# Column sums of squares on TensorE: one result column instead of 128, in a three-layer fp32 transformer kernel

## The reference

```python
def rms_norm(x, g):
    xf = x.astype(jnp.float32)
    y = xf * lax.rsqrt(jnp.mean(xf * xf, axis=-1, keepdims=True) + EPS)
    return (y * g.astype(jnp.float32)).astype(x.dtype)

# second model, each of its six sub-layers:
        h = rms_norm_2(x, g[0])
        ...
        x = x + rms_norm_2(y, g[1])
```

## Time and profile before

| | before |
|---|---|
| median of 3 runs | 2448.61 us (2446.7 to 2450.1) |
| profiled execution, its own time | 2450.1 us |
| profiled execution, span of the trace | 2448.3 us |
| mean granted TensorE clock | 0.957 |
| PE busy | 2257.6 us, 92% |
| weight loads (PEld) busy | 1836.5 us, 75% |
| DVE, ACT, POOL busy | 51%, 46%, 28% |
| mean DMA rate | 106 GB/s |

### The profile page before, as it was taken

One profiled execution on the slowest core, in us unless ns is written; L12 is line 12 of the kernel. 1 busy time (PEld: TensorE's weight loads), 2 busy tenths in 40 slices (PEclk: granted clock), 3 DMA queues, 4 the chain that ended last, 5 costly groups with the idle time before them and its releaser, 6 DMA issues.

```text
span 2448.3 us, 30850 instructions
## 1 busy us (share of the span) xinstructions
PE 2257.6 (92%) x11314; PEld 1836.5 (75%) x11314; DVE 1240.1 (51%) x2222; ACT 1118.1 (46%) x1958; POOL 680.1 (28%) x434
## 2 busy tenths in 40 slices
PE   7988899989999999988979999999987888999997
PEld 5755688867888887766867888887875777788886
DVE  6767544537999834455454322224538445323233
ACT  5445633446888725555343322223737334332221
POOL 4150033311000121401233332233922323332232
PEclk9888999989999999998989999999999889999999
DMA  4300022215999720220211322221310221223221
GB/s 159 112 18 35 10 99 97 101 47 190 391 391 384 290 86 19 75 88 1 86 61 52 104 96 95 102 95 61 104 69 1 69 70 35 95 95 104 95 95 52
DMA packets 71653, 258.92 MB, mean 106 GB/s; under 512 B 7952, under 2 KB 8080, under 8 KB 71120
## 3 DMA queue, kind: packets, MB, share of 16 engines
q1 hardware_dynamic: 66816, 238.76, 27.4%
q0 software_dynamic: 2816, 11.82, 1.3%
q10 hardware_dynamic: 1872, 6.37, 0.7%
HBM read 245.36 MB, written 11.56 MB: 105 GB/s over the span
## 4 chain that ended last, share of the span: by engine, by line
PE 78%; DVE 8%; ACT 6%; issue 4%; POOL 2%; DMA 1%; POOLq 0%; DVEq 0%; SPq 0%; ACTq 0%
PE ps L506 16%; PE ps L508 16%; PE ps L507 16%; PE ps L1108 3%; PE ps L566 3%; PE ps L1123 2%; PE ps L2669 2%; PE ps L2671 2%; PE ps L2670 2%; PE ps L542 2%; PE ps L548 2%; PE ps L543 2%; PE ps L1142 2%; PE ps L2696 1%; PE ps L2697 1%
## 5 line engine op out<-in xcount | busy, mean ns | idle before, releaser
L448 ACT ACTIVATE wh<-raw 128x1024 fp32r<-128x1024 f32 x308 | 322.4, 1055 | 484.8 <-PE ps L508 458.4
L453 DVE TENSOR_TENSOR wl<-raw,wh 128x1024 fp32r<-128x1024 f32 x180 | 242.5, 1354 | 539.8 <-ACT wh L448 533.8
L506 PE MATMUL ps<-hh,wh 128*128 128x512 f32 (+1 forms) x1192 | 469.4, 394 | 8.2 <-POOL wl L453 7.9
L508 PE MATMUL ps<-hh,wl 128*128 128x512 f32 (+1 forms) x1192 | 466.2, 391 | 0.0
L507 PE MATMUL ps<-hl,wh 128*128 128x512 f32 (+1 forms) x1192 | 466.2, 391 | 0.0
L453 POOL TENSOR_TENSOR wl<-raw,wh 128x1024 fp32r<-128x1024 f32 x128 | 309.2, 2416 | 553.0 <-ACT wh L448 543.7
L506 PE MATMUL ps<-act,wh 128*128 128x512 f32 (+1 forms) x688 | 269.5, 392 | 11.5 <-ACT act L1368 9.9
L506 PEld LDWEIGHTS ps<-hh,wh 128*128 128x128 f32 (+1 forms) x1192 | 225.0, 189 | 57.8 <-issue 10.5
L507 PE MATMUL ps<-act,wh 128*128 128x512 f32 (+1 forms) x688 | 267.4, 389 | 0.0
L508 PE MATMUL ps<-act,wl 128*128 128x512 f32 (+1 forms) x688 | 267.2, 388 | 0.0
L508 PEld LDWEIGHTS ps<-hh,wl 128*128 128x128 f32 (+1 forms) x1192 | 224.7, 189 | 47.9
(11 more groups left out here) (463 smaller groups left out, 3908.4 us busy)
## 6 DMA issues: line engine op xcount, KB each, us to landing
raw<-d_w SPq DMA_DIRECT2D x277, 512.0 KB
raw_x<-d_moe SPq DMA_DIRECT2D x84, 512.0 KB, 6.8
raw<-d_moe SPq DMA_DIRECT2D x84, 512.0 KB
d_xs<-Sb POOLq DMA_DIRECT2D x7, 514.0 KB, 7.6
Xb<-d_xs ACTq DMA_DIRECT2D x6, 514.0 KB, 6.4
area<-d_mem POOLq DMA_DIRECT2D x3, 1024.0 KB, 5.2
d_ys<-rows ACTq DMA_DIRECT2D x6, 512.0 KB, 6.2
xT<-d_x SPq DMA_DIRECT2D x8, 256.0 KB, 7.0
```

What stands on the lines that cost most here:

```text
L448: me.e.activation(hi, raw, ACT.Copy).then_inc(*me.done("wh", m))
L453: me.e.tensor_tensor(lo, raw, hi.bitcast(F32), ALU.subtract).then_inc(*me.done("wl", m))
L506: me.e.matmul(bank[0:m, 0:n], wh[:, c], hi, start=k == 0, stop=False)
L508: mm = me.e.matmul(bank[0:m, 0:n], wl[:, c], hi, start=False, stop=last)
```

## The change

`column_sums` multiplies by one column of ones (or, for two heads, by columns 0 and 64 of the block matrix) instead of 128 columns, and writes its sums side by side at the start of the PSUM bank, one column for each tile of 128 tokens (or two). `summed_columns`, which picked every 128th or 64th column, is gone; its three readers read the first columns of the bank. The number of matmuls, their stationary operands, their waits and the semaphores they raise are the same, and so is the order of instructions on every engine.

```diff
 def column_sums(K, me, acc, sq, key, first, last, rows=128, ncol=T, nh=1):
     nt = ncol // 128
-    rhs = K.ones[0:rows, :] if nh == 1 else K.blk
+    rhs = K.ones[0:rows, 0:1] if nh == 1 else K.blk[:, 0:128:64]
     for i in range(nt):
-        q = slice(128 * i, 128 * i + 128)
-        mm = me.e.matmul(acc[:, q], sq[0:rows, q], rhs, start=first and i == 0, stop=last and i == nt - 1)
+        mm = me.e.matmul(acc[:, nh * i:nh * i + nh], sq[0:rows, 128 * i:128 * i + 128], rhs, start=first and i == 0,
+                         stop=last and i == nt - 1)
     mm.then_inc(*me.done(*key))
-
-
-def summed_columns(acc, ncol=T, nh=1):
-
-    return acc[:, 0:ncol:128 // nh]
...
-    me.e.activation(s, summed_columns(acc, ncol, nh), ACT.Sqrt, bias=K.eps, scale=1.0 / width).then_inc(*me.done("root", st))
+    me.e.activation(s, acc[:, 0:ncol // 128 * nh], ACT.Sqrt, bias=K.eps, scale=1.0 / width).then_inc(*me.done("root", st))
...
-    me.e.activation(K.stat[:, i, 0:NQ], summed_columns(K.ACC), ACT.Sqrt, bias=K.eps, scale=1.0 / D).then_inc(*me.done("root", st))
+    me.e.activation(K.stat[:, i, 0:NQ], K.ACC[:, 0:NQ], ACT.Sqrt, bias=K.eps, scale=1.0 / D).then_inc(*me.done("root", st))
...
-    me.e.scalar_tensor_tensor(v.rearrange("p (i h) -> p i h", h=nh), summed_columns(acc, T, nh).rearrange("p (i h) -> p i h", h=nh),
+    me.e.scalar_tensor_tensor(v.rearrange("p (i h) -> p i h", h=nh), acc[:, 0:NQ * nh].rearrange("p (i h) -> p i h", h=nh),
                               1.0 / width, bc(K.et[:, :], nh), ALU.mult, ALU.add).then_inc(*me.done("var", st))
```

## The result

The changed kernel took 2468.69 us (median of 4 runs, 2460.8 to 2470.8), the kernel before beside it 2447.65 us (2440.45 to 2450.1). The ratio is 1.0070, 95% interval 1.0043 to 1.0098. So one result column instead of 128 costs 17 to 20 us by the two ratios. The forecast was 2485 us, 36 us slower, with a range of 2455 to 2503: the direction and the mechanism came as forecast, the size at about half.

What follows compares the result with a forecast made beforehand. The prediction took PE to bound the kernel (busy 92% of the span, 78% of the chain). Pace 0, train ends -2 and clock +38.3 gave +36.3 us on the median 2448.61, so 2485 us, range 2455 to 2503.

Steps and rivals of the forecast that it cites:

- Pace: Term for the 700 matmuls of column_sums: loads set 0.112 us a record at any width, so 0 us gained.
- The far end, 73 us: Most hopeful end of the pace term: the line's whole 3% of the chain, up to 73 us, would go.
- End of a train: Term for each sum's last matmul: ready 0.107 us earlier, 2 us taken off in all.
- The clock, the mechanism: Claim that PE, though busy, loses its clock some 3 us into a train of narrow matmuls.
- The clock, the count: Claim of one clock fall for each of the 15 norms, among trains of 24, 16 and 40 records.
- The clock, the price: Claim that each fall costs half its low time, mean 2.55 us, so 15 falls add 38.3 us.
- The rival of the held clock: PE's clock holds in all trains, leaving only the train ends: 2446.6 us, chance 0.11.
- The rival of the long trains: Clock falls only at the three trains of 40, 3.4 us each: 2456.8 us, chance 0.13.
- Cheaper matmuls: Rival: columns set the pace of column_sums after all, half of 73 us goes: 2412 us, chance 0.04.

Runs made afterwards that it cites:

- e7: Kernel before (128 columns) with POOL adding squares of one more chunk, four calls of column_sums per norm instead of five: 2431.29 us, ratio 0.9946.
- e8: Kernel before with three of four tiles left out of the sums of chunks 4 to 6, 270 records gone: 2429.22 us, ratio 0.9936.
- e1: Kernel before with 64 moving columns in column_sums instead of 128: 2452.62 us, ratio 1.0028.
- e2: Kernel before with 16 moving columns in column_sums instead of 128: 2458.82 us, ratio 1.0054.
- e4: Changed kernel with the three calls of each 24-record train set apart by at least 3 wide matmuls: 2448.71 us, ratio 1.0013 to the kernel before.
- e13: The changed kernel run again, unaltered, against the kernel before: 2466.96 us, ratio 1.0082.
- e6: Kernel before with one column only in the three norms whose sums stand as 40 records in a row: 2444.61 us, ratio 1.0008.
- e3: Changed kernel with 128 columns again in the first three column_sums calls of each norm: 2450.61 us, ratio 1.0032 to the kernel before.
- e9: Kernel before (128 columns) with POOL adding squares of two more chunks, three calls of column_sums per norm instead of five: 2443.94 us, ratio 0.9990.
- e10: e7 with one column instead of 128, early trains of 16 records: 2457.82 us, ratio 1.0058 to the kernel before.

## Where the prediction was right and where not, step by step

*Pace.* Right. A train of 24 took 2.68 us and takes 2.72, the end of it already at low clock; one of 40 took 4.48 and takes 4.37. Within trains at full clock the records start 111 or 112 ns apart in both kernels; only the first gap is shorter, 26 ns against 108. The far end, 73 us, was never there; e7 and e8 show that it takes fewer records, not narrower ones.

*End of a train.* Right in kind: 4.48 to 4.37 is 0.11 us at one train. (The 168 ns that I took for 4 columns belong to a record with 2; with 4 the shortest is 169.) I took 2 us off. PE's work at full clock fell by 5.2 and 5.9 us in the two profiles; part of that may be how records that overlap are counted, and no run separates it.

*The clock, the mechanism.* Right. Falls stand in or right behind narrow trains with PE busy throughout; they get fewer as the columns come back (one of the twelve pairs in e1's profile, eight in e2's), and at most of the norms' trains they go when wide matmuls are set between (e4).

*The clock, the count.* Too high, though the total of low time came out. In the profile of after, 8 of the twelve pairs that stand in wide work lost their clock where they had not, 4 kept it (the trains at 26.8, 867, 1318 and 2434); in e13's the first lost it too. I had counted all twelve and the three trains of 40, behind which the clock was low before as well and now is for 10.2 us in place of 6.8. The mean clock of its first twelve runs, 0.944, makes 275 us at low clock (2 x 0.056 x 2462), against 201 us in the 35 runs of before: 74 us more. I had put in 15 falls of 5.1 us, 76 us. That the two agree is in good part luck: in the profile two of the eight pairs, with low stretches of 23.9 us at 564.6 and 20.5 us at 2008.5, hold 27.3 of the 58.1 us that came on top.

*The clock, the price.* This is the step that failed: 15 falls at 2.55 us, 38.3 us, from "so a low stretch costs half its length in work", applied to every low microsecond and with nothing taken off behind it. 74 us of low clock would have cost 37; the kernel paid 17 to 20. Record against record, from the start of each of the 15 trains to 15 us behind it, the two profiles of the changed kernel fall behind by 17.6 and 23.2 us in sum, and part of that is taken back later. Three things stood in place of the price. First, PE is idle in part of the low time: in the profiles 58.1 us more of low clock (201.4 to 259.5) held 50.8 us more of busy PE (between the first and the last matmul). Second, what PE lost it did not wait for later: 9.4 us of its idle time went, at the routing, at the inverse of two norms and in an attention. I had named the routing and left it at nothing, and had written that PE "is on the chain in all 15 places, so a slower PE is a longer kernel". It is on the chain there, but at the next such point it waited less. Third, the 5 us of work that ended sooner. A fall in the middle of wide work cost 1.6 us at four of the eight pairs, about the lower of my two prices, which I had from a stretch behind a wait (1272.9) and not behind a narrow train. The routing's cost 4.5 us, the one at 1241 nothing in the end, and the mean of the eight is 1.9. At trains of 40 it was 0.8 us or less by 30 us behind their start. My mean of 2.55 was above these, but below the 6.2 us of the first pair in e13's profile: a train of 16 that falls into low time takes 3.21 us there where it took 1.78.

*The rival of the held clock* is out: 17 to 20 us, not -2. *The rival of the long trains* had a total of 8 us, half of the result, by the wrong places: e6 shows 2 us (5 at most) at these three, e3 12 us at the early trains. *Cheaper matmuls* is out by the pace.

## What to carry to other kernels

If a matmul's pace is set by the load of its stationary operand, a narrower moving operand gains 0.1 us a train and nothing for each record in it; count records and cut those (e7: 120 records fewer, 13.4 us), as long as what replaces them is in time (e9: 240 fewer, no gain, since PE waited 3 to 4 us at a time and lost its clock by it). Narrow matmuls in a row let TensorE's clock fall though the engine is never idle; if they must be narrow, set wide ones between them (e4: 0.1% in place of 0.8%). And price a fall by what PE would have waited for behind it: only the low time that no later wait takes up costs its half.

## What the runs showed of the hardware that I had not expected

The mean granted clock of this kernel fell by degrees with the columns of its sums: 0.959, 0.953, 0.947 and 0.944 at 128, 64, 16 and 1 columns, with every record at the same 0.11 us. Half-empty trains of 64 columns already cost 0.28% (0.07 to 0.48). And trains of 16 narrow records, which kept their clock at 1210.39 in the changed kernel, lose it at some places where two stand near each other: e10's one column cost 26.5 us over e7, more than the 20 us of the changed kernel with its trains of 24. The comparison starts from different clocks: e7 had 0.964, better than the kernel before, and e10 has 0.943, as the changed kernel has (0.944 and 0.942). So the narrow sums took back what e7 had gained in clock as well. Why the clock of e10 is no higher than that of the changed kernel, with shorter trains and fewer falls at the pairs, is open; e10 had 5 runs (2453.59 to 2461.08), and none took its parts apart.
